# Rounding each weight tile with one instruction and taking its rest with one, in a split-precision encoder layer

## The reference, cut to what matters

```python
xn = _rmsnorm(x, norm_pre_w[l])                     # x: 256 tokens x 2048 channels, float32
h = xn @ w_in[l]                                    # 2048 x 13312
... neighbourhood attention branch o_a, HGRN2 branch o_b, gates g_a, g_b ...
y = g_a * (o_a @ w_branch[l, :NA_WIDTH]) + g_b * (o_b @ w_branch[l, NA_WIDTH:])
x = x + _rmsnorm(y @ w_out[l], norm_post_w[l])
```

## Time and profile before

| what | value |
|---|---|
| median of 3 runs | 809.37 us (809.16 to 809.92) |
| the profiled execution: its time | 809.55 us |
| its span, first to last instruction | 807.8 us |
| PE busy (matmul) | 795.5 us, 98% of the span |
| PE weight loads busy | 688.9 us, 85% |
| DVE busy | 626.7 us, 78% |
| ACT busy | 391.5 us, 48% |
| GpSimd busy | 25.3 us, 3% |
| moved by DMA | 155.62 MB, mean 193 GB/s |
| mean granted TensorE clock | 0.998 of full |

### The profile page before, as it was taken

How to read it: one execution, slowest core, us unless ns; L and a number is a source line. 1 busy time by engine, 2 the same in 40 slices (tenths; PEclk the granted TensorE clock), 3 DMA queues, 4 the chain that set the end, 5 groups by cost and what they waited for, 6 DMA issues and landing times.

```text
span 807.8 us, 13847 instructions
## 1 busy us (share of the span) xinstructions
PE 795.5 (98%) x5638; PEld 688.9 (85%) x5638; DVE 626.7 (78%) x1080; ACT 391.5 (48%) x666; POOL 25.3 (3%) x45
## 2 busy tenths in 40 slices
PE   8999999999999999999999999999999999999996
PEld 6888888888888888888888888888888888888884
DVE  5777658889889889889889889889875787865543
ACT  6655444444544444445445445445445555454442
POOL 4000000000000000000000000000000000000002
PEclk9999999999999999999999999999999999999999
DMA  9966497766766666657657657657567676586522
GB/s 329 394 216 206 117 239 199 195 171 180 193 167 187 191 162 192 190 158 199 182 157 206 176 159 211 170 162 204 158 175 201 203 204 180 187 305 215 187 74 105
DMA packets 239104, 155.62 MB, mean 193 GB/s; under 512 B 3904, under 2 KB 219968, under 8 KB 238400
## 3 DMA queue, kind: packets, MB, share of 16 engines
q1 hardware_dynamic: 237888, 150.49, 64.4%
q10 hardware_dynamic: 1152, 4.24, 1.4%
HBM read 151.56 MB, written 2.10 MB: 190 GB/s over the span
## 4 chain that ended last, share of the span: by engine, by line
PE 96%; DMA 1%; SPq 1%; POOL 0%; ACT 0%; DVE 0%; issue 0%; POOLq 0%; ACTq 0%
PE psum L1138 47%; PE psum L1146 25%; PE psum L1367 3%; PE psum L1369 3%; PE psum L1368 3%; PE psum L1200 3%; PE psum L1201 3%; PE psum L1202 3%; PE psum L1243 1%; DMA raw<-in_w_in 1%; PE psum L1277 1%; PE psum L1229 1%; PE psum L1266 1%; PE psum L1216 0%; SPq L352 0%; POOL big L437 0%
## 5 line engine op out<-in xcount | busy, mean ns | idle before, releaser
L688 DVE TENSOR_TENSOR w_lo<-raw,w_hi 128x1024 fp32r<-128x1024 f32 x268 | 317.6, 1220 | 66.8 <-ACT w_hi L453 66.6
L1138 PE MATMUL psum<-act_hl,w_hi 128*128 128x512 f32 x1408 | 335.9, 391 | 0.0
L1138 PEld LDWEIGHTS psum<-act_hl,w_hi 128*128 128x128 f32 x1408 | 258.9, 188 | 50.0
L453 ACT ACTIVATE w_hi<-raw 128x1024 fp32r<-128x1024 f32 x268 | 270.7, 1053 | 61.3 <-PE psum L1202 27.6
L1146 PE MATMUL psum<-act_hl,w_lo 128*128 128x256 f32 x1408 | 185.5, 285 | 0.0
L1146 PEld LDWEIGHTS psum<-act_hl,w_lo 128*128 128x128 f32 x1408 | 178.1, 191 | 4.8
L467 ACT ACTIVATE part<-psum 128x256 f32<-128x256 f32 x88 | 33.6, 382 | 227.4 <-PE psum L1146 227.4
L1138 PE MATMUL psum<-branch_hl,w_hi 128*128 128x512 f32 x256 | 61.4, 391 | 0.7 <-DVE branch_hl L888 0.7
L1138 PEld LDWEIGHTS psum<-branch_hl,w_hi 128*128 128x128 f32 x256 | 47.0, 188 | 10.1 <-issue 1.1
L1367 PE MATMUL psum<-w_hi,act_hl 128*128 128x512 f32 x128 | 49.9, 390 | 0.0
L1368 PE MATMUL psum<-w_lo,act_hl 128*128 128x512 f32 x128 | 49.8, 389 | 0.0
(11 more groups left out here) (126 smaller groups left out, 615.4 us busy)
## 6 DMA issues: line engine op xcount, KB each, us to landing
raw<-in_w_in SPq DMA_DIRECT2D x102, 1024.0 KB, 5.8
raw<-in_w_branch SPq DMA_DIRECT2D x16, 1024.0 KB, 5.9
raw<-in_w_out SPq DMA_DIRECT2D x16, 1024.0 KB, 5.1
raw<-in_w_in SPq DMA_DIRECT2D x8, 256.0 KB, 5.8
big<-in_x_rows SPq DMA_DIRECT2D x2, 1024.0 KB, 15.0
big<-in_x_rows ACTq DMA_DIRECT2D x2, 1024.0 KB, 6.0
big<-in_x_turned SPq DMA_DIRECT2D x7, 256.0 KB, 7.4
bias<-in_band_bias SPq DMA_DIRECT2D x8, 192.0 KB, 5.9
```

The costliest lines, as they stand in the source:

```text
L453: nc.scalar.activation(w_hi[:, (2 * r + h) % HALVES, :], raw[:, r, 1024 * h:1024 * (h + 1)], ACT.Copy).then_inc(hi_ready, 1)
L688: nc.vector.tensor_tensor(w_lo[:, i, :], raw[:, r, 1024 * h:1024 * (h + 1)], w_hi[:, i, :].bitcast(F32), ALU.subtract).then_inc(lo_ready, 1)
L1138: nc.tensor.matmul(sums[h][:, :], w_hi[:, i, w], operand[:, k, :], start=k == 0 if whole else k % 8 == 0, stop=False, skip_group_check=True)
```

## The change

For every tile from tile 4 on (132 tiles), `split_tile` on ACT and `split_tile` on DVE issue one instruction over 2048 columns each, where they issued two over 1024. The order of everything else stays. The rounding now waits for both halves of tile n-2 at once, the subtraction for both halves of `hi_ready`, and both counters go up by two at the end of the one instruction.

```diff
             def split_tile(n, r, landed):
-                split_hi(n, r, landed, 0)
-                split_hi(n, r, landed, 1)
+                act.wait_ge(raw_landed[r], landed)
+                wait(act, half_used, n * 2 - HALVES + 2)
+                i = 2 * r % HALVES
+                nc.scalar.activation(w_hi[:, i:i + 2, :].rearrange("p h c -> p (h c)"), raw[:, r, :],
+                                     ACT.Copy).then_inc(hi_ready, 2)
...
             def split_tile(n, r):
-                split_lo(n, r, 0)
-                split_lo(n, r, 1)
+                dve.wait_ge(hi_ready, n * 2 + 2)
+                i = 2 * r % HALVES
+                nc.vector.tensor_tensor(w_lo[:, i:i + 2, :].rearrange("p h c -> p (h c)"), raw[:, r, :],
+                                        w_hi[:, i:i + 2, :].rearrange("p h c -> p (h c)").bitcast(F32),
+                                        ALU.subtract).then_inc(lo_ready, 2)
```

## The result

| | before | changed |
|---|---|---|
| median | 809.26 us (809.09 to 809.92, 4 runs) | 814.65 us (813.42 to 814.89, 4 runs) |
| profiled execution | 809.55 us, span 807.8 | 814.89 us, span 813.2 |
| mean granted TensorE clock | 0.998 | 0.994 |

The ratio is 1.0061, with an interval of 1.0048 to 1.0073. The change makes the kernel slower by 5.4 us; the forecast was 3.3 us, and the median lies 0.55 us above 814.1, the upper end of the range.

The account below looks back on a forecast made before the run. PE was taken to bound the kernel; only output-stage waits cost, 1.94 us at O1 plus 1.44 at O5, O9 and O13, 3.38 in all, giving 812.7 us, range 812.3 to 814.1.

Parts of the forecast that it names:

- what bounds the kernel: Whole kernel: the chain that ends last is 96% PE, so busy time saved on ACT and DVE is worth nothing.
- O5, O9 and O13: Output-stage tiles rounded after ACT squares two blocks: PE waits 0.36 us plus 0.12 restart each, 1.44 us in all.
- The tightest place of the input stage: Last piece of `act_hl`, needed by PE at 96.06: forecast to end at 95.75, leaving 0.3 us, no wait.
- the prices: Extrapolated times of one 2048-column instruction: 2290 ns for DVE's subtraction, 1925 ns for ACT's rounding.
- O1's wait: Output stage, second tile: ready at 719.80 instead of 717.86, so PE stands idle 1.94 us longer.
- The handover from ACT to DVE: Inside a merged tile: DVE starts 1.955 us after ACT's start, 1.925 for the rounding plus 0.03.
- rival 4: Output stage: TensorE's clock falls after about 2.0 us idle in front of O1, costing 2.7 us more, 815.4; chance 0.04.
- Rival 3: Group stage: DVE's lag piles up and PE waits in each group, 6.4 us more, 819.1 us; chance 0.06.
- The 0.8 us of lag: Group stage: each subtraction ends 0.81 us later than before, delaying DVE work queued behind it, at no cost to PE.
- The wait that was to empty the lag: Group stage: DVE's wait of 1.21 us at 296.17, said to empty the lag once in each group.
- the room of 2.6 us: Scan's early session in the groups: last input ends at 329.3, PE reads it at 331.91, leaving 2.6 us.

Follow-up runs that it names:

- the repeated kernel: The changed kernel itself, run once more without any edit: 815.06 us.
- O1 alone: Kernel before with only the second tile of the output stage (O1) merged: 811.56 us, ratio 1.0036.
- O5 alone: Kernel before with only the output-stage tiles O5, O9 and O13 merged: 811.46 us, ratio 1.0023.
- ACT alone: Only ACT's rounding merged, DVE's subtraction still in halves as in the kernel before: 810.69 us, ratio 1.0008.
- the changed order: Changed kernel, all tiles merged, with O1, O5, O9 and O13 split ahead of the other work: 809.06 us, ratio 0.9995.
- extra-work runs: Merged kernel with the four tiles split earlier, plus an extra DVE subtraction per group tile: 512 columns 813.51 us, 840 columns 840.04 us.

## Why the prediction was right or wrong

**Right: what bounds the kernel, and where it costs.** DVE's and ACT's saved 10 and 13 us were worth nothing. PE waits for a merged split in front of O1, O5, O9 and O13 and nowhere else; the run with these four in halves takes the time of before. The tightest place of the input stage came out as forecast:

```profile
95.13 0.68 DVE L995 TENSOR_TENSOR act_hl<-hg,act_hl 128x512 fp32r<-128x512 f32 x1
```

It ends at 95.81, forecast 95.75, and PE takes it at 96.07 without a wait: 0.26 us were left of the 0.3 forecast.

**Right: the prices and O1's wait.** 2290 and 1925 ns were forecast, 2291 and 1911 were measured. O1: 1.94 us forecast, 2.02 measured. The handover from ACT to DVE took 2.02 us from ACT's start, not 1.955. I had taken the 0.03 us from a 1024-column row; behind the long rounding it is 717.39 - 715.37 - 1.92 = 0.10 us.

**Too small: O5, O9 and O13.** 0.48 us each was forecast, 0.63 to 0.65 measured. 0.07 us is that handover. 0.05 us is ACT's start, 1.35 us behind the first square (737.98 to 739.33) instead of 1.30. The rest, some 0.03 us, I haven't traced. Together 0.48 us of the miss. The range's upper end had room for it.

**Wrong: the clock.** The step that failed is the clock, which the sum put at nothing: rival 4 had a chance of 0.04, for something that then happened in 12 of 19 executions with this wait. Its price was too high, 2.7 us for 1.6 measured, and its cause was named rightly. I held two rows against it: a wait of about 1.5 us in front of tile 2 with the clock at 1.00, and the clock still full four us after PE's last matmul. The first was a single execution with a shorter wait, where even the longer one spares 7 of 19. The second I read as though the clock fell only after more than four us of idle time. But what the clock is granted at a moment answers to what PE did before it: in the two traces with the fall it came 1.4 and 0.3 us after PE had resumed. A row that shows the clock full during a pause, then, does not speak for the time behind the pause. The profiled execution of the changed kernel shows it once more at the start, with a gap of 1.5 us, where the trace of before has 1.0:

```profile
7.00:8.00 1.00, 1.00 (x4) 0.88 1.04 318
8.00:9.00 1.00, 1.00 (x3) 0.50 0.97 348
```

It costs nothing there: the trace of before has a wait of 1.5 us in front of tile 2, the slow matmuls take the place of that wait, and tile 2 starts at 19.44 instead of 19.35. So pauses of the same length, 1.5 us, went with a fall here and with none in front of tile 2 in the trace of before; the length alone doesn't decide. (At the very start the column of the granted clock needs care: in the traces of the repeated kernel, O1 alone, O5 alone, ACT alone and the changed order, matmuls between 6 and 10 us start 0.43 us apart, though it says 1.00.) The Trainium skill, "TensorE: Matmul & The Clock Gate", section "HAM oscillation — how this bites in real kernels", warns that a wait for input can send PE back to half rate, and I weighed that too lightly. The traces agree, and differ in three points: the waits of the page's example are longer, some 3 to 5 us by its figure, where 1.9 us of idle time was enough here; the page has the clock fall within the wait, where here it fell behind it; and here it fell in part of the executions only.

**Right: the groups.** Rival 3 did not come about. The 0.8 us of lag was measured as 0.77 at the critical operation. The wait that was to empty the lag does so: it shrinks from 1.21 us to 0.35, and the operation behind it starts at 296.14 where it started at 296.17:

```profile
296.14 0.56 DVE L719 SCALAR_TENSOR_TENSOR wide<-psum,bias 128x384 f32<-128x384 f32 x1 [0.35 <-PE psum L1249]
```

The extra-work runs show, though, that the room of 2.6 us that I named would not have borne even 0.6 us of work for each tile.

**The sum:** 1.94 + 1.44 = 3.38 forecast; 2.02 + 1.92 + 1.61, less 0.15, = 5.40 measured in the profiled execution. The miss is 2.02 us: 1.61 the clock, 0.48 O5, O9 and O13, 0.08 O1, less 0.15. An execution without the fall would have been near the forecast: the one at 813.42 us is inside the range.

## What to carry to other kernels

Joining two halves of a producer's work saves its fixed cost, but where a second engine and then PE take the halves in turn, it lengthens the way to the first usable half by half a tile on each of them; look for the few tiles that have other work in front of them, which alone paid here, and move that work behind. A delay that only shifts a start does not grow from step to step, while work added to an engine without idle time does: set the first against the room at one place, and the second, summed, against it. And when a change opens a gap of two us in PE's stream, price the half-rate stretch behind it too, with a real chance and not a small one.

## What was not expected of the hardware

- The granted clock fell to its half level after PE had resumed from a gap of 2.27 us between matmul starts, 1.4 us behind the restart in one trace and 0.3 us in another. Both times it stayed there for 3.4 us, though PE was busy throughout, and cost 1.6 us. By their times 12 of 19 executions had it, and none of 16 with a gap of 1.1 us or one partly filled.
- With four small matmuls on constants inside such a wait, 1.05 us of PE's time, none of five executions had the fall, and the median was 1.0 us lower.
